# RWKV-7 triangular inverse with the identity inside its scores, its side work spread over more levels, and a new order at the end of the S5 layer

## The reference

```python
def wkv7(r, w, k, v, z, b):               # RWKV-7, state (heads, 64, 64)
    def step(state, inp):
        r_t, w_t, k_t, v_t, z_t, b_t = inp
        sa = einsum('bhvk,bhk->bhv', state, z_t)
        state = state * w_t + sa[..., None] * b_t + v_t[..., None] * k_t
        return state, einsum('bhvk,bhk->bhv', state, r_t)

def odd_mixer(xn, w_in, ..., D, w_glu):   # S5 layer
    u = xn @ w_in
    ...                                   # complex scan over time, 64 groups of 16 channels
    y = gelu(y + D * u)
    val, gate = split(y @ w_glu, 2)
    return val * sigmoid(gate)
```

## Time and profile before

| | us |
|---|---|
| median of 3 runs | 2760.04 (2758.92 to 2761.87) |
| the profiled execution, its own time | 2760.72 |
| its span, first to last instruction | 2758.5 |
| PE busy in the span | 2622.4 (95%) |
| DVE, ACT, POOL busy | 1301.3, 934.0, 879.3 |
| from issue to landing, median: `g_in`, GLU weights | 5.0, 2.8 |

### The profile page before, as it was taken

How to read it: one execution, slowest core, us unless ns; L and a number is a source line. 1 busy time by engine, 2 the same in 40 slices (tenths; PEclk the granted TensorE clock), 3 DMA queues, 4 the chain that set the end, 5 groups by cost and what they waited for, 6 DMA issues and landing times.

```text
span 2758.5 us, 35785 instructions
## 1 busy us (share of the span) xinstructions
PE 2622.4 (95%) x13567; PEld 2180.1 (79%) x13567; DVE 1301.3 (47%) x1572; ACT 934.0 (34%) x1420; POOL 879.3 (32%) x781
## 2 busy tenths in 40 slices
PE   6999799999799999999999999979999999999998
PEld 4778588888577887888788888868878888888886
DVE  5532277676434556564564435642244413431443
ACT  3442354454433322343343334412233212221333
POOL 4222234333232223575572221222222222222221
PEclk7999899999899999999999999989999999999999
DMA  2111000000012211243251134621111111111112
GB/s 86 44 46 49 20 1 1 1 1 1 13 45 58 58 44 58 64 144 106 65 175 58 46 99 163 202 79 50 47 41 49 50 50 46 49 49 46 49 46 84
DMA packets 239923, 164.57 MB, mean 60 GB/s; under 512 B 23981, under 2 KB 227271, under 8 KB 237767
## 3 DMA queue, kind: packets, MB, share of 16 engines
q1 hardware_dynamic: 225344, 141.37, 17.1%
q10 hardware_dynamic: 14471, 21.74, 2.2%
HBM read 129.51 MB, written 29.36 MB: 58 GB/s over the span
## 4 chain that ended last, share of the span: by engine, by line
PE 62%; issue 5%; DVE 2%; POOL 2%; ACT 1%; DMA 0%; ACTq 0%; SPq 0%; POOLq 0%; DVEq 0%
PE acc_o L1556 53%; PE acc_o L1805 4%; POOL dense_lo L374 1%; PE bank_a L2705 1%; PE bank_b L2728 1%; PE bank_b L2458 1%; PE bank_b L2463 1%; PE bank_a L2449 1%; POOL c_lo L2567 0%; DVE val L2038 0%; PE acc_o L2105 0%; POOL t_gx L2381 0%; POOL t_mg L2374 0%; DVE fine L2222 0%; ACT u_now L2807 0%
## 5 line engine op out<-in xcount | busy, mean ns | idle before, releaser
L374 POOL TENSOR_TENSOR dense_lo<-dense_raw,dense_hi 128x512 fp32r<-128x512 f32 x324 | 427.7, 1320 | 1200.4 <-ACT dense_hi L367 1199.1
L367 ACT CAST dense_hi<-dense_raw 128x512 fp32r<-128x512 f32 x324 | 192.4, 594 | 778.3 <-PE acc_o L1556 719.2
L1556 PE MATMUL acc_o<-a_hi,dense_hi 128*128 128x512 f32 x1328 | 413.9, 393 | 8.2 <-POOL a_lo L2573 4.6
L1556 PE MATMUL acc_o<-a_hi,dense_lo 128*128 128x512 f32 x1328 | 410.7, 391 | 0.0
L1556 PE MATMUL acc_o<-a_lo,dense_hi 128*128 128x512 f32 x1328 | 410.5, 390 | 0.0
L1556 PE MATMUL acc_o<-c_hi,dense_hi 128*128 128x512 f32 x1096 | 340.1, 392 | 22.9 <-POOL dense_lo L374 20.7
L1556 PE MATMUL acc_o<-c_lo,dense_hi 128*128 128x512 f32 x1096 | 338.2, 390 | 0.0
L1556 PE MATMUL acc_o<-c_hi,dense_lo 128*128 128x512 f32 x1096 | 338.1, 390 | 0.0
L1556 PEld LDWEIGHTS acc_o<-a_hi,dense_hi 128*128 128x128 f32 x1328 | 247.2, 189 | 62.1 <-POOL a_lo L2573 5.8
L1556 PEld LDWEIGHTS acc_o<-a_hi,dense_lo 128*128 128x128 f32 x1328 | 250.2, 188 | 52.5
L1556 PEld LDWEIGHTS acc_o<-a_lo,dense_hi 128*128 128x128 f32 x1328 | 250.1, 188 | 52.5
(11 more groups left out here) (382 smaller groups left out, 3776.4 us busy)
## 6 DMA issues: line engine op xcount, KB each, us to landing
dense_raw<-in_f_w_up SPq DMA_DIRECT2D x176, 256.0 KB, 3.0
dense_raw<-in_f_w_down SPq DMA_DIRECT2D x72, 256.0 KB, 2.9
w_raw_e<-in_e_w_in SPq DMA_DIRECT2D x44, 256.0 KB, 2.9
s_states<-t_hx ACTq DMA_DIRECT2D x16, 512.0 KB, 3.0
g_in<-s_inputs SPq DMA_DIRECT2D x8, 1024.0 KB, 5.0
hx<-s_states SPq DMA_DIRECT2D x8, 1024.0 KB, 5.3
dense_raw<-in_o_w_glu SPq DMA_DIRECT2D x32, 256.0 KB, 2.8
s_inputs<-t_in ACTq DMA_DIRECT2D x14, 512.0 KB, 2.7
```

Source lines behind the costliest of these rows:

```text
L367: nc.scalar.copy(self.hi[:, par, 0:n, :], self.raw[:, par, 0:n, :]).then_inc(w_hi_done, 1)
L374: pool.tensor_tensor(self.lo[:, par, 0:n, :], self.raw[:, par, 0:n, :], self.hi[:, par, 0:n, :].bitcast(F32), op=ALU.subtract).then_inc(w_ ...
L1556: last = nc.tensor.matmul(acc[:, h * HALF:(h + 1) * HALF], w[:, chunk, j, :], x[:, k + j, h * HALF:(h + 1) * HALF], start=first, stop=final)
```

## The change

- `level_mask` of levels 1 to 6 gets the identity added, and so does `a_zb`. The masked product then holds the identity, and the two products of `close_pe` give the new X whole. The 12 identity products of group 0 in a chunk (512 columns each) go, and so does `add_old` for group 1: DVE's x1 becomes a copy, and the transpose of group 1 (xt1) is copied by ACT.
- `a_zb` is made by POOL (an addition) ahead of `first_pool`; ACT made it with two copies.
- The side work moves: ACT's logarithm stays at level 3 and its exponential goes to level 4, the second half of `exps_act` to level 5; DVE's `zr_dve` goes from level 5 to 6 and `r_dve` behind level 6; POOL's `b_pool` comes ahead of `out_pool`.
- S5 end: the weight places take chunks of units 0, 1 and 2 in the order 0, 1, 2 (first halves), 0, 1, 2 (second halves), unit 2 in `bank_a`; states of step 7 come ahead of the output of step 6, with the read of their inputs earlier on SP; all `a_lo` are made by DVE; half of the moves of step 5 go to ACT's queue.

```diff
@@ masks_dve @@
+                    link.run(nc.vector.tensor_tensor(level_mask[:, 1:LEVELS, :], level_mask[:, 1:LEVELS, :],
+                                                     ident[:, :].unsqueeze(1).to_broadcast([P, LEVELS - 1, P]), ALU.add))
@@ close_pe @@
-                up(add4(banks[g][1], x_inv_t[g], MX_AT[g], None if g else x_inv[g]), f"x_ps{g}")
-                up(add4(banks[g][2], mx[g], XT_AT[g], None if g else x_inv_t[g]), f"x_ps{g}")
+                up(add4(banks[g][1], x_inv_t[g], MX_AT[g]), f"x_ps{g}")
+                up(add4(banks[g][2], mx[g], XT_AT[g]), f"x_ps{g}")
@@ level_act @@
                 up(nc.scalar.copy(x_inv_t[0][:, :, :], psum4(banks[0][2])), "xt0")
+                wait(act, "x_ps1", c, 2 * k + 1)
+                up(nc.scalar.copy(x_inv_t[1][:, :, :], psum4(banks[1][2])), "xt1")
@@ close_dve @@
-            add_old(c, x_inv[1][:, :, :], banks[1][1], "x1")
-            wait(dve, "x_ps1", c, 2 * k + 1)
-            add_old(c, x_inv_t[1][:, :, :], banks[1][2], "xt1")
+            up(nc.vector.tensor_copy(x_inv[1][:, :, :], psum4(banks[1][1])), "x1")
@@ a_zb_pool, new @@
+            for g in range(2):
+                wait(pool, "a_kept", c, 3 + g)
+                wait(pool, f"mx_ps{g}", c, LEVELS - 1, back=1)
+                ptt(pool, a_zb[g][:, :, :], a_b[g][:, :, 0, :],
+                    ident[:, :].unsqueeze(1).to_broadcast([P, RT, CH]), ALU.add, "a_zb")
@@ S5 end, SP @@
+                    if i == DT - 2:
+                        move_y(sp, i - 1, (0,))
+                        read_inputs(i + 1)
+                        move_y(sp, i - 1, (1,))
...
                 move_y(sp, DT - 2, (2, 3))
                 move_y(sp, DT - 1, (2, 3))
-                with sp.Fori(1, DT) as i:
+                load_unit(DT + 2)
+                dn.load(sp, w_glu, DT, glu_cols(1, 1), u_glu + 3, 0)
+                with sp.Fori(2, DT) as i:
@@ S5 end, PE @@
                 states_pe(DT - 2)
+                pe.wait_ge(unit_free, u_glu + 1)
+                place_products(pe, 0, 0, 2, g_ready)
                 filters_pe(DT - 2)
+                states_pe(DT - 1)
+                place_products(pe, 0, 2, 4, g_ready).then_inc(w_used, 1)
                 output_pe(DT - 2)
+                pe.wait_ge(unit_free, u_glu + 2)
+                place_products(pe, 1, 0, 4, g_ready).then_inc(w_used, 1)
                 filters_pe(DT - 1)
                 output_pe(DT - 1)
+                pe.wait_ge(s5_dve, 15 * (DT - 1) + 5)
+                place_products(pe, 2, 0, 4, g_ready).then_inc(w_used, 1)
+                place_products(pe, 3, 4, 8, g_ready).then_inc(w_used, 1)
+                place_products(pe, 4, 4, 8, g_ready).then_inc(w_used, 1)
+                place_products(pe, 5, 4, 8, g_ready).then_inc(w_used, 1)
@@ S5 end, ACT (gelu_act of steps 6 and 7 also issues the first half of their moves) @@
+                move_y(act, DT - 3, (2, 3))
+                keep_hi(5)
+                hi_place(act, 2)
                 gelu_act(DT - 2)
+                hi_place(act, 3)
                 keep_hi(6)
                 gelu_act(DT - 1)
+                hi_place(act, 4)
                 keep_hi(7)
+                hi_place(act, 5)
```

More of the change, by code:

```diff
@@ L794, in trunk @@
             "dve": {"biased": 2, "logsum": 4, "mids": 1, "k2": 2, "k_floor": 1, "y_floor": 1, "kk": 1, "zr": 2,
[L795 removed]
+                    "ends": 1, "bonus": 1, "a_kept": 8, "first": 2, "mx0": 6, "mx1": 6, "x1": 7, "res1": 1,
                     "x_t0": 1, "x_t1": 1, "state_mid": 1, "state": 2, "gn": 1},
[L797 removed]
+            "pool": {"v_now": 1, "a_zb": 2, "kk_raw": 1, "centred": 2, "rk": 2, "bk": 3, "first_t": 2, "out": 4},
         })
@@ L952, in grow_pe, with add4 @@
                 up(last, f"mx_ps{g}")
-        def add4(bank, lhs, rhs_at, old=None):
-            if old is not None:
-                units(bank, eye, old, start=True, stop=False)
+        def add4(bank, lhs, rhs_at):
             for i in range(RT):
-                last = beside_zeros(bank, i, lhs[:, i, :], rhs_at + i, start=old is None and i == 0, stop=i == RT - 1)
+                last = beside_zeros(bank, i, lhs[:, i, :], rhs_at + i, start=i == 0, stop=i == RT - 1)
             return last
@@ L1110, in turn_act @@
             up(nc.scalar.copy(by_token[:, n, :], prep_ps[n % 2][:, :]), "turned_kept")
-        def a_zb_act(act, c):
-            for g in range(2):
-                wait(act, "a_kept", c, 3 + g)
-                wait(act, f"mx_ps{g}", c, LEVELS - 1, back=1)
-                up(nc.scalar.copy(a_zb[g][:, :, :], a_b[g][:, :, 0, :]), "a_zb")
         def level_act(act, c, k):
@@ L1418, in turn_of_pool @@
                 raw_pool(pool, c + 1)
+            a_zb_pool(pool, c)
             first_pool(pool, c)
@@ L2561, in trunk, with load_place, hi_place, lo_place @@
         glu_out = sem("glu_out")
-        POOL_TILES = 7
+        PLACES = ((0, 0), (1, 0), (2, 0), (0, 1), (1, 1), (2, 1))
+        def load_place(sp, n):
+            unit, chunk = PLACES[n]
+            sp.wait_ge(w_lo_done, 2 * u_glu + n + 1)
+            sp.dma_start(dn.raw[:, n % 2, :, :],
+                         w_glu[:, KC * chunk:KC * chunk + KC, glu_cols(unit // 2, unit % 2)]).then_inc(w_loaded[n % 2], 16)
+        def hi_place(act, n):
+            act.wait_ge(w_loaded[n % 2], 16 * (u_glu + n // 2) + 16)
+            act.wait_ge(w_used, 2 * u_glu + n + 1)
+            nc.scalar.copy(dn.hi[:, n % 2, :, :], dn.raw[:, n % 2, :, :]).then_inc(w_hi_done, 1)
+        def lo_place(pool, n):
+            pool.wait_ge(w_hi_done, 2 * u_glu + n + 1)
+            pool.tensor_tensor(dn.lo[:, n % 2, :, :], dn.raw[:, n % 2, :, :], dn.hi[:, n % 2, :, :].bitcast(F32),
+                               op=ALU.subtract).then_inc(w_lo_done, 1)
+        def place_products(pe, n, first, end, g_ready):
+            unit, chunk = PLACES[n]
+            pe.wait_ge(w_lo_done, 2 * u_glu + n + 3)
+            for k in range(first, end):
+                last = tile_products(dn, pe, DT, a_hi, a_lo, unit, k, g_ready, n % 2, glu_acc(unit))
+            return last
+        def wait_place(eng, n):
+            eng.wait_ge(w_used, 2 * u_glu + n + 3)
+        def glu_acc(unit):
+            return bank_a if unit == 2 else dn.acc[unit % 2]
+        def inputs_done(i):
+            return 3 * i + (1 if i < DT - 1 else 0)
+        def filters_done(i):
+            return 3 * i + 2
+        def outputs_done(i):
+            return 3 * i + (4 if i == DT - 2 else 3)
         def y_part(eng, k, done):
```

137 lines of the change are left out of this document (67 added, 70 removed).

## The result

The changed kernel takes 2737.36 us (median of 4 runs, 2734.55 to 2739.57), against 2760.56 for the kernel before, run on the same chip. The ratio is 0.9917, 95% interval 0.9903 to 0.9932: faster by 23 us, where 41 were forecast, and 1.4 us above the end of the range at 2736. The profiled run took 2735.16 us and its span is 2733.4, 25.1 less than the 2758.5 of before.

A forecast was written before the change was run, and what follows sets the result against it. PE, busy 95%, was taken as bound by a PE, DVE, PE chain in RWKV levels and by waits and slow matmuls at S5's end; 19.9 + 21.0 = 40.9 us off 2760.0 gives 2719, range 2704 to 2736.

The forecast's parts named there:

- What is hidden: Start of an RWKV chunk: POOL's a_zb additions ahead of first_pool, 1.46 us per operation, cost nothing, with 0.6 us cover.
- rival 3: Start of RWKV chunks: POOL's four operations slowed beside DVE's two-SBUF-input operations, 3.1 us or more each; kernel slower; chance 0.03.
- RWKV, levels: RWKV middle chunk, close to close: 25.8 us now, 23.4 after, so 2.4 us a chunk less.
- The loss at level 2 to 3: RWKV level 2 to 3: y_sum waits for ACT's centred_act behind xt1; 4.28 us becomes 4.89, a loss of 0.6.
- The table loads: ACT in RWKV: separate loads, 1.28 us each, stay ahead of logarithm and exponential, though the skill says one suffices.
- Rival 1: ACT's three copies a level hold RWKV: 2729 if four levels come 0.3 us later, 2739 if all gain goes; chance 0.17.
- S5's end: New order of tiles, states and outputs at the end of S5: 21.0 us less, bounds 16 to 25.
- the two waits forecast: End of S5: PE waits 3 us ahead of the last tile 7 and another 3 us ahead of unit 3.
- with 5 us to landing: End of S5: g_in, issued at 1787.2, lands 5 us later, so states 7 end at 1796.0.
- The one loss of 2.7 us to the clock: End of S5: the two new PE waits together cost one slow-clock loss of 2.7 us.
- Rival 4: The order at S5's end gives only half, as transfers crowd (clock low, g_in late): 2730; chance 0.10.
- RWKV's bounds: RWKV's gain of 19.9 us: nothing if ACT holds every level, 35 us if nothing is held.

The follow-up runs named there:

- zb_behind_first: The changed kernel with one more wait: POOL's a_zb begins only when DVE's two first masks are done; 2724.52 us (0.9867 of the kernel before).
- s5_alone: The kernel before with only the change's new order at the end of S5, RWKV as before; 2743.96 us (ratio 0.9936).

## Why the prediction was wrong

**The step that failed** is in "What is hidden", and in rival 3 with it. Both asked whether POOL's operations would be late because of DVE. The rows of `first_pool` that I leaned on the earlier trace rows show POOL's side, and there the count held: POOL's four operations took 5.9 us as counted (2.95 and 2.96), and no mask of level 1 waited for them. What I did not ask was what POOL does to DVE; that term was put at nothing. DVE is the engine on the path at the start of a chunk: behind the two first masks stand a_k, x1, the sigmoids' inputs and the masks of level 1. Rival 3 had the right two engines, the right place and the right condition (two SBUF inputs), but put the price on the wrong one of them, and a bound of 3.1 us per operation on it. The price was 0.89 us on each of 16 masks, 14.2 us. Without it RWKV gives 19.4 us by the medians (`zb_behind_first` against `s5_alone`, four times each), where 19.9 were forecast; by the traces it is 17.0 (the last exponential at 725.32, and at 742.35 before).

The Trainium skill's sentence (GPSIMD Engine Reference, "1. Specifications": the SBUF interfaces are shared with VectorE, with contention where VectorE has two SBUF inputs) speaks of both engines. The trace agrees with it, at 1570 ns instead of 683. I had set it aside with the argument that the masks already ran beside `first_pool`. They did, but only the second of a pair, and it was under way when POOL began.

**RWKV, levels.** Right in sum and in the causes of the waits, with some luck in the sum. Close to close it is 4.5, 4.7, 3.7, 3.8, 4.5 and 2.3 us by the starts of the rows, for 4.41, 4.89, 3.42, 3.85, 4.92 and 1.90 forecast from where the array is free. Single levels are off by up to 0.4 us, in both directions, and this cancels: counted alike, the sums are 23.1 and 23.4. The loss at level 2 to 3 was right in cause; it was 0.4 us and not 0.6 (4.7 for the 4.28 of before).

**The table loads.** Right: in the trace of the changed kernel too one stands ahead of the logarithm (508.33) and one ahead of the exponential (512.14), 1.28 us each. The order printed ahead of the prediction shows only the first of them.

**Rival 1** (ACT holds RWKV) gave 2729 to 2739, and the result lies there, but not by its mechanism, so the number is no support for it: with POOL's additions put later ACT's long wait shrank by itself.

**S5's end.** The order of things was right: the two waits forecast are there (2.62 and 2.14 us for 3 and 3), tiles 0 and 1 run at once, scan 7 is hidden. The term that was mis-sized is "with 5 us to landing": 8.3. Its row was right for the kernel before, where `g_in` was issued 11.8 us behind `hx`; in the new order `hx` (1024 KB) and two weight tiles are issued 4.2 and 3.8 us ahead and were still on their way. `g_in` came 3.3 us later than counted, and this brought a third wait of PE with slow matmuls behind it, which the sum did not have. The one loss of 2.7 us to the clock was the other rough term: the trace has two of 1.6, at states 7 and at unit 3. Waits and losses together are 11.6 us where the sum had 8.7. I forecast 21.0; the part alone gave 16.6 by the medians, and with `hx` behind `g_in` (5.4 more) it would be 22.0; the traces, read from the start of states 6, have 17.6 and 21.1. Rival 4 named this mechanism ("`g_in` late"), with 0.10 and 10 us.

**The range.** It ended 1.4 us short of the result. Two failures of one sign came together, 11.7 us in RWKV and 4.4 in S5. I gave RWKV's bounds as nothing to 35, and then let the range leave out the lower part, for the bad cases were priced one at a time. With both put right, the medians give 2760.6 - 19.4 - 22.0 = 2719.2, and the traces 2760.6 - 17.0 - 21.1 = 2722.5. No kernel with just these two edits was run, so this is a sum of differences, good to a few us, and that the first comes out at the forecast's own number is luck. But it shows that the rest of the arithmetic stood, and that the two durations taken over from the kernel before did not.

## What to carry to other kernels

When an operation moves to GpSimd, ask first what VectorE does in the same microseconds, and cost the change on VectorE: here its masks, with both inputs in SBUF, seem to have stood still as long as GpSimd's operation lasted. Put the GpSimd operation behind it, or beside operations that read PSUM; one wait was worth 8 to 13 us here. A landing time holds only for what is ahead of the transfer: when an order moves issues, list the large transfers of the last few microseconds and put those that are needed later behind.
